# Four gate rows: products and copies replaced by a DMA round trip, and two chunks of the modulation summed later

## The reference

```python
mod = (c_act @ ada_w[layer] + ada_b[layer])[:, None, :]
sh_a, sc_a, gt_a, sh_m, sc_m, gt_m = jnp.split(mod, 6, axis=-1)
h = modulate(rms_norm(x, attn_norm[layer]), sh_a, sc_a)
...   # mix = diff_attention (layer 0) or nsa_attention, the sparse one (layer 1)
x = x + gt_a * mix
h = modulate(rms_norm(x, mlp_norm[layer]), sh_m, sc_m)
x = x + gt_m * squared_relu_mlp(h, mlp_w1[layer], mlp_w2[layer])
```

## Time and profile before

| | |
|---|---|
| median of 3 runs | 1310.14 us (1309.81 to 1311.36) |
| the profiled execution | 1312.58 us, span 1310.8 us |
| busy share PE / DVE / ACT / POOL | 96% / 66% / 53% / 10% |
| `m0` | about 172 to 343 us |
| sparse attention, blocks 0 to 18 | about 430 to 515 us |
| DMA | 267.38 MB, mean 204 GB/s |

### The profile page before, as it was taken

How to read it: one execution, slowest core, us unless ns; L and a number is a source line. 1 busy time by engine, 2 the same in 40 slices (tenths; PEclk the granted TensorE clock), 3 DMA queues, 4 the chain that set the end, 5 groups by cost and what they waited for, 6 DMA issues and landing times.

```text
span 1310.8 us, 21652 instructions
## 1 busy us (share of the span) xinstructions
PE 1262.0 (96%) x8368; PEld 1095.4 (84%) x8368; DVE 860.9 (66%) x1501; ACT 691.7 (53%) x1219; POOL 137.1 (10%) x154
## 2 busy tenths in 40 slices
PE   7999899999999999999999989999999999999999
PEld 5887799888799656899898867999998778899997
DVE  6588699997675675786546774665565566654444
ACT  3566553444455665645445874644444565654542
POOL 1022111211100000101100320100100100010100
PEclk9999999999999999999999999999999999999999
DMA  9979379999489142585553532685554554466550
GB/s 366 388 240 346 120 274 353 356 352 347 137 244 288 50 177 65 184 319 181 191 172 108 176 94 81 158 315 183 172 181 141 176 178 137 154 184 198 179 161 33
DMA packets 123781, 267.38 MB, mean 204 GB/s; under 512 B 11040, under 2 KB 33824, under 8 KB 123296
## 3 DMA queue, kind: packets, MB, share of 16 engines
q1 hardware_dynamic: 119328, 257.23, 59.2%
q0 software_dynamic: 1728, 6.29, 1.5%
q10 hardware_dynamic: 2624, 2.49, 0.6%
HBM read 264.83 MB, written 1.15 MB: 203 GB/s over the span
## 4 chain that ended last, share of the span: by engine, by line
PE 63%; DVE 5%; ACT 3%; issue 2%; POOL 1%; DVEq 0%; ACTq 0%; POOLq 0%
PE bank L538 12%; PE bank L540 11%; PE bank L539 11%; PE ps_s L538 3%; PE ps_s L539 3%; PE ps_s L540 3%; PE ps_p L539 3%; PE ps_p L538 3%; PE ps_p L540 3%; PE ps_s L1326 1%; DVE wlo L1621 1%; PE ps_p L1169 1%; PE ps_p L1145 1%; POOL rs L3446 1%; PE ps_s L1133 1%
## 5 line engine op out<-in xcount | busy, mean ns | idle before, releaser
L1621 DVE TENSOR_TENSOR wlo<-wring,whi 128x1024 fp32r<-128x1024 f32 (+1 forms) x376 | 457.9, 1227 | 265.4 <-ACT whi L2767 261.0
L2767 ACT ACTIVATE whi<-wring 128x1024 fp32r<-128x1024 f32 (+1 forms) x376 | 388.3, 1045 | 364.0 <-PE bank L540 132.2
L538 PE MATMUL bank<-h_hi,whi 128*128 128x256 f32 (+1 forms) x1224 | 348.8, 285 | 5.7 <-DVE wlo L1621 2.6
L539 PE MATMUL bank<-h_lo,whi 128*128 128x256 f32 (+1 forms) x1224 | 346.2, 283 | 0.0
L540 PE MATMUL bank<-h_hi,wlo 128*128 128x256 f32 (+1 forms) x1224 | 346.1, 283 | 0.0
L538 PEld LDWEIGHTS bank<-h_hi,whi 128*128 128x128 f32 (+1 forms) x1224 | 234.0, 191 | 11.9 <-issue 10.1
L539 PEld LDWEIGHTS bank<-h_lo,whi 128*128 128x128 f32 (+1 forms) x1224 | 234.1, 191 | 0.8
L540 PEld LDWEIGHTS bank<-h_hi,wlo 128*128 128x128 f32 (+1 forms) x1224 | 234.1, 191 | 0.0
L3462 POOL TENSOR_TENSOR ex<-ex 128x512 f32<-128x512 f32 x64 | 82.1, 1285 | 670.7 <-ACT g_hi L2898 670.5
L538 PE MATMUL ps_s<-whi,g_hi 128*128 128x512 f32 x256 | 101.2, 395 | 2.5 <-DVE wlo L1621 2.5
L538 PE MATMUL ps_p<-whi,g_hi 128*128 128x512 f32 x256 | 100.5, 393 | 0.0
(11 more groups left out here) (391 smaller groups left out, 1773.5 us busy)
## 6 DMA issues: line engine op xcount, KB each, us to landing
wring<-in_mlp_w SPq DMA_DIRECT2D x128, 512.0 KB, 5.3
wring<-in_mlp_w_in SPq DMA_DIRECT2D x64, 512.0 KB, 3.8
wring<-in_mlp_w_out SPq DMA_DIRECT2D x64, 512.0 KB, 4.1
wring<-in_ada_w_t SPq DMA_DIRECT2D x48, 512.0 KB, 8.0
wring<-in_ada_w SPq DMA_DIRECT2D x36, 512.0 KB, 5.8
wring<-in_moba_w_qkv SPq DMA_DIRECT2D x24, 512.0 KB, 4.0
wring<-in_a_qk SPq DMA_DIRECT2D x16, 512.0 KB, 9.2
wring<-in_kv_ada_w_t SPq DMA_DIRECT2D x16, 512.0 KB, 7.4
```

Source lines behind the costliest of these rows:

```text
L538: nc.tensor.matmul(out, lh, rh, start=first, stop=False, skip_group_check=mixed)
L539: nc.tensor.matmul(out, lh, rl, start=False, stop=False, skip_group_check=mixed)
L1621: v.tensor_tensor(piece_view(wlo, p), raw_view(p), piece_view(whi, p).bitcast(F32), ALU.subtract).then_inc(lo_ready, 1)
L2767: a.activation(piece_view(whi, p), raw_view(p), ACT.Copy).then_inc(hi_ready, 1)
```

## The change

It has two parts.

1. **The gate rows.** The products of `gate_rows` and the copies are gone from PE, DVE and ACT. In their place ACT issues `gate_out`: a DMA of the 8 columns of `mod`, 32 bytes from each of 128 partitions, to a DRAM scratch of 128 x 8 numbers. POOL issues `gate_load`: a DMA that reads the scratch as one run of 1024 numbers and writes it to all 128 partitions of `gate_row` (512 KB). The row then lies in the order (p, j), feature 128 j + p at place 8 p + j. `residual` and `y_residual` read it as `q (p j) -> q j p`: 4 runs of 128 numbers that stand 32 bytes apart.
2. **Two chunks moved.** The chunks 4 and 5 of `ada1` (the gate of the sparse attention) leave the list of weights of `m0` and DVE's pieces 40 to 47 there. They come as eight single loads between the loads behind `b_in`, and DVE sums the blocks in the sparse attention: two in block 0, one in each of the blocks 1 to 6, behind the block's weighting. Their neighbours are laid out anew: before, the list has four loads of `b_out`, eight of `ada_by_rows`, four of `b_out`; now two of `b_out`, the eight in halves among the sums' loads, then the rest.

```diff
-    plan += mix(mlp("m0"), ada(0, range(10, 12)) + ada("kv", range(4)) + ada(1, range(6)))
+    plan += mix(mlp("m0"), ada(0, range(10, 12)) + ada("kv", range(4)) + ada(1, range(4)))
...
-    for tag, lo, hi in (("b_out", 0, 2), ("b_out_mid", 2, 3), ("b_out_end", 3, 4)):
-        plan += [((tag, c[0][1]),) + c[1:4] + (c[4][lo:hi],) for c in b_out]
-        plan += ada_by_rows(1, range(8, 10)) if lo == 0 else []
+    gate_parts = [c[:4] + (c[4][j:j + 1],) for c in ada(1, range(4, 6)) for j in range(4)]
+    row_halves = [c[:4] + (c[4][j:j + 2],) for c in ada_by_rows(1, range(8, 10)) for j in (0, 2)]
...
+    plan += gate_parts[:2] + out_part["b_out", 0] + gate_parts[2:4]
+    for i in range(4):
+        plan += row_halves[i:i + 1] + (out_part["b_out", 1] if i == 3 else []) + gate_parts[4 + i:5 + i]
+    plan += [c for tag in ("b_out_mid", "b_out_end") for i in range(2) for c in out_part[tag, i]]
...
-        drain_order = [ada_order[c] for c in opening + CHUNKS[:2] + ROWS[:1] + CHUNKS[2:] + ROWS[1:]] + ada_order[10:]
+        drain_order = [ada_order[c] for c in opening + CHUNKS[:2] + ROWS[:1] + CHUNKS[2:] + ROWS[1:]] + ada_order[10:20]
+        drain_order += ada_order[22:24] + ada_order[20:22] + ada_order[24:]
...   # PE: gate_rows and its four calls are gone
...   # DVE
+            def gate_half(n):
+                return gate_row[:, :].rearrange("q (p j) -> q j p", j=KT)[:, 4 * n:4 * n + 4, :]
...
-                    v.tensor_tensor(tmp[:, n, :], src, gate_row[:, n * W:(n + 1) * W], ALU.mult).then_inc(drained[b], 1)
+                    v.tensor_tensor(tmp[:, n, :].rearrange("q (j p) -> q j p", p=P), src.rearrange("q (j p) -> q j p", p=P),
+                                    gate_half(n), ALU.mult).then_inc(drained[b], 1)
...
             def gate_use(name):
-                for g in range(2):
-                    bank_emptied(dve, (name, "gate", g))
+
+                dve.wait_ge(sem("gate_in"), 16 * (GATES.index(name) + 1))
...
-            mlp("m0", ada_order[10:22], last=lambda: (gate("m0"), gate_use("m0")))
+            mlp("m0", ada_order[10:20], last=lambda: gate_use("m0"))
...   # blocks of the sparse attention, behind nsa_weigh
+                for n in range(b + (b > 0), b + 2 if b < 7 else 0):
+                    matvec(ada_order[20 + n // 4], n % 4)
-                if b == 4:
-                    gate("n1")
...   # ACT: at b == 7 of m0 and m1, in slot 7 of a0, at b == 10 of the sparse attention
+            def gate_out(name):
+
+                first = gate_column[name]
+                act.wait_ge(mod_drained, drained_by(first // 4, first // 4 + 1))
+                a.dma_start(gate_scratch[GATES.index(name)], mod[:, first:first + KT]).then_inc(sem("gate_out"), 16)
...   # POOL: before the square 9 of m0 and m1, behind the roots of ("diff", 6) and ("kv", 1)
+            def gate_load(name):
+
+                i = GATES.index(name)
+                pool.wait_ge(sem("gate_out"), 16 * (i + 1))
+                if i:
+                    pool.wait_ge(x_ready, 4 * i)
+                g_.dma_start(gate_row[:, :], gate_scratch[i:i + 1].rearrange("a p j -> a (p j)").to_broadcast(
+                    [P, D])).then_inc(sem("gate_in"), 16)
```

More of the change, by code:

```diff
@@ L620, in by_token @@
                     piece_over(last, uses_[1] if end else None)
-            def gate_rows(name, first):
-                pe.wait_ge(mod_drained, drained_by(first // 4, first // 4 + 1))
-                for g in range(2):
[L626 to L633, removed]
             def attention(name, units, q_parts, pairs, v, dv, beside=None):
@@ L1047, in turn_inside @@
                     turn_scaled("kv", 0)
-            mlp("m0", lambda: gate_rows("m0", 40), inside=turn_inside)
+            mlp("m0", inside=turn_inside)
             late_rows(3)
@@ L1314, in turn_second @@
                 return step
-            mlp("m1", before_last=lambda: gate_rows("m1", 64 + 40), inside=turn_first("l", 12))
+            mlp("m1", inside=turn_first("l", 12))
             def head_scores(name, u, parts):
@@ L1901, in y_residual @@
                 if gated:
-                    link(v.tensor_tensor(tmp[:, n, :], y, gate_row[:, n * W:(n + 1) * W], ALU.mult))
+                    link(v.tensor_tensor(tmp[:, n, :].rearrange("q (j p) -> q j p", p=P), y.rearrange("q (j p) -> q j p", p=P),
+                                         gate_half(n), ALU.mult))
                     settle()
@@ L2456, in bias_steps @@
                         drained[uses[("bias2", s)][0]], 1)
-            mlp("m1", ada_order[26:28], other=late_constants, last=lambda: (gate("m1"), gate_use("m1")), first=8)
+            mlp("m1", ada_order[26:28], other=late_constants, last=lambda: gate_use("m1"), first=8)
             dve.wait_ge(sem("final_in"), 16)
@@ L2888, in mlp @@
                 for b in range(2 * FF // W):
+                    if b == 7 and tag in GATES:
+                        gate_out(tag)
                     key = (f"{tag}_w1", b // 2, b % 2)
@@ L3016, in _ @@
                 if s == 7:
-                    for g in range(2):
-                        drain(("a0", "gate", g), gate_row[:, g * W:(g + 1) * W], (0, W))
+                    gate_out("a0")
                 if slot_head(s - 3) is not None:
@@ L3127, in _ @@
                     q_drain(3)
+                if b == 10:
+                    gate_out("n1")
                 if b in (5, 7):
@@ L3456, in chunk_load @@
                 g_.dma_start(chunk_buffers[n % 2], src).then_inc(sem(f"chunk_in{n % 2}"), 16)
+            def gate_load(name):
[5 more added lines that the diff above has]
+                    [P, D])).then_inc(sem("gate_in"), 16)
             def squares(tag):
                 for b in range(2 * FF // W):
+                    if b == 9 and tag in GATES:
+                        gate_load(tag)
                     pool.wait_ge(sem("mlp_ghi"), 16 * int(tag[1]) + b + 1)
@@ L3471, in _ @@
                 roots(k)
+                if k == rstd_at[("diff", 6)]:
+                    gate_load("a0")
+                if k == rstd_at[("kv", 1)]:
+                    gate_load("n1")
                 if rstd_at[("diff", 0)] <= k < rstd_at[("diff", 4)]:
```

14 lines of the change are left out of this document (5 added, 9 removed).

## The result

| | before | changed |
|---|---|---|
| median | 1309.97 us (4 runs, 1308.57 to 1311.36) | 1326.50 us (4 runs, 1324.50 to 1327.61) |
| ratio | 1 | 1.0125, 95% interval 1.0104 to 1.0146 |
| profiled execution | 1312.58 us, span 1310.8 | 1324.50 us, span 1322.7 |

The change makes the kernel 16.5 us slower; the forecast was 1309.2 with a range from 1303.0 to 1317.5. I explain the 11.9 from the traces and let the medians of the experiments speak for the rest.

What follows compares the result with a forecast made beforehand. The prediction took PE as the bound (busy 96% of the span, 63% of the chain of waits). Its terms, -5.5 - 3.1 + 7.7 = -0.9, gave 1311.7 against 1312.6 profiled, 1309.2 against the median; range 1303.0 to 1317.5.

Steps and rivals of the forecast that it cites:

- Gate products and copies: `a0`, `m0`, `m1`: removed gate calls give 1.9, 1.7 and 1.7 us, DVE's copies 0.2; 5.5 us less.
- The DMA round trip: Gate write and load: taken as 0, since rows are wanted long after; in `m0`'s full queue 1.5 us more waiting.
- What `m0` gets back: Last third of `m0`: fewer loads and sums remove waits and slow clock, 4.6 less 1.5 for the gate load; 3.1 us less.
- What the sparse attention pays: Sparse attention: first blocks, late loads, slow clock, last sum and a DMA issue; 7.7 us more in all.
- Blocks 0 to 4: Sparse attention: the removed gate call gives 1.7, the sums cost 1.3 and 0.8 of lag; net +0.4 us.
- The wait at block 4: End of block 4, sparse attention: ACT's splits wait for later-issued `b_out` loads; PE goes on 4.8 us later, +0.4 included.
- the clock ... I take 1.5 for both: Sparse attention: slow clock behind PE's standing in block 1 to 2 and block 5; 1.5 us, range 0 to 3.6.
- Nothing in blocks 5 and 6 gives it back: Sparse attention: PE is the path on both sides, so the delay from block 4 stays.
- The last sum in block 6: Sparse attention: the sum stands between the weighting and the low part PE's mix needs; 1.2 us more.
- Strided reads: The 16 gated products: DVE reading `gate_row` 32 bytes apart costs nothing; 0 us, judged from L2240's PSUM read.
- The rival: Gated products: the strided read costs a pass, 0.56 us on 13 of 16, 7.3 in all, giving 1316.5; chance 0.24.

Runs made afterwards that it cites:

- e6: Only the first part (gates by DMA in 32-byte runs, chunks stay in `m0`), read contiguously so features get other features' gates; 1304.72 us, ratio 0.9958 to the kernel before.
- e2: Only the first part, with the scratch written in feature order by 4-byte writes so DVE reads contiguously; 1315.55 us, ratio 1.0036 to the kernel before.
- e7: Whole change, strided, `b_out`'s loads early as in e4, and the last two sums moved from blocks 5 and 6 to 7 and 8; 1311.86 us, ratio 1.0016.
- e1: Only the first part of the change: gates by DMA in 32-byte runs, read strided, weights list and sums as before; 1312.61 us, ratio 1.0020 to the kernel before.
- e12: As e7, but the gate row read contiguously (gates of other features); 1307.27 us, ratio 0.9979 to the kernel before.
- e3: The whole change with the scratch written by 4-byte writes so the row is read contiguously; 1326.32 us, ratio 1.0124 to the kernel before.
- e5: The whole change, written in 32-byte runs but read contiguously (gates of other features); 1317.75 us, ratio 1.0051 to the kernel before.
- e9: The whole change, each gate read at another distance: 16 bytes in `a0`, 64 in `m0`, 8 in `n1`, 128 in `m1`; 1321.59 us, ratio 1.0085.
- e4: The whole change, strided, with two loads of `b_out` placed ahead of the eight loads of rows; 1319.26 us, ratio 1.0075 to the kernel before.
- e8: Whole change, strided, loads around `b_out` listed as before, the eight sums in blocks 8 to 15, gate written at block 16; 1312.24 us, ratio 1.0020.
- e10: First part alone, PE turning gate columns to rows, ACT copying and writing 512-byte runs, contiguous reads; 1315.28 us, ratio 1.0034 to the kernel before.
- e11: As e10, with ACT's two copies in `m0` and `m1` moved behind the activations of block 8; 1307.18 us, ratio 0.9979 to the kernel before.

## Why the prediction was wrong

**Gate products and copies** (forecast -5.5): right. The calls gave 2.05, 1.9 and 1.5 us, and e6, 5.3 under the kernel before, has this term, the call of `n1` and the gate's load in it.

**The DMA round trip** (0, and 1.5 in `m0`): right for runs of 32 bytes; no product waited for its row; the 1.5 was not measured by itself. I had bounded the write by a few us of lateness. What it can cost was elsewhere: with 4-byte runs it held the queue of `m0` for 8 us (e2).

**What `m0` gets back** (-3.1): right in the trace, -3.4 between 241.84 and 307.95. But e7 is no better than e1 by more than 0.8, and e12 no better than e6, so in the median it hardly reached the end.

**What the sparse attention pays** (+7.7): the mechanism was right and its size was not. Blocks 0 to 4 (+0.4) were right: PE lost 2.1 us to the sums and the call gave 1.6 back. The wait at block 4 is as forecast (4.7 of ACT, 5.1 of PE between blocks 2 and 5, against 4.8). The step that failed is "the clock ... I take 1.5 for both": it is 5.4, since PE ran 12 us at half its clock behind the wait. e3, e5 and e9 have a like wait (5.0 to 5.5 us) and lose 5 to 6 us by the clock behind it. I had scaled it from the 1.8 behind a wait of 1.95, where the slow stretch is short, to a wait of 4.9. The bound that I gave from above, 3.6, was too low as well. "Nothing in blocks 5 and 6 gives it back" held. The last sum in block 6 (+1.2) did not show, since PE was late by then anyhow; when e4 took the first wait away it came up as a wait of 5.1, because its load was late, where I had priced its work alone.

**Strided reads** (0): wrong, and the largest error: 8 to 9 us by e5 and e6. The step that failed is "I take 0", by the row that was nearest, L2240, which reads PSUM. It was no neighbour: another memory. The rival had the right mechanism and nearly the right price (0.56 a product, measured 0.42 to 0.45; 7.3 in all, measured 8.8), and 0.24 for it was too little, since its only counter-evidence was that row. Its total is close in part by luck: 13 products of 0.42 to 0.45 are only 5.5 to 5.9 us, and the clock behind the products, which it left out, makes up more where it falls: 1.5 us behind each of two residuals in the changed kernel, none there in e1.

The Trainium skill's page that the prediction cites was the better guide. Page "SBUF — State Buffer", section "Specifications (TRN2)", asks for at least two hits in a line of 16 bytes for full bandwidth. Here the traces agree: at 8 bytes two numbers fall into a line and the product takes 0.69, at 16 one does and it takes 1.07. The note in section "Door 1: The DMA port swizzle", which the prediction drew on and which calls a distance of four fp32 numbers free, doesn't agree with the 1.07.

**The sum.** With 8.8 for the stride and 5.4 for the clock the forecast's own terms give 1309.2 + 8.8 + 3.9 = 1321.9. The rest to 1326.5, 4.6 us, I can't place in full. If the 3.1 of `m0` is left out, since it hardly reached the end in the median, the terms give 1325.0. And 1.6 us in the changed kernel's trace are a stretch of half clock in the latent attention (0.57 from 796 to 800 us). e2, e3, e5, e7, e8 and e10 have such a stretch some 20 to 30 us earlier in the same stage; e1, e4, e6, e9, e11, e12 and the kernel before have none. Nothing in that stage was changed. What starts it stays open.

## What to carry to other kernels

A row bounds an operand only in its own memory: where the layout of an SBUF operand changes and no row shows it, give the skill's rule for that memory the larger chance, or measure the one instruction first. Where a change reorders an in-order load queue, look for each load that moved behind a later release, and for what stands behind the engine that wants it; price a wait of PE of 5 us at one and a half times to twice its length (5.1 became 7.5 in e4, and about 10 in the changed kernel). When an experiment takes a cost away by another route, look whether that route has a price of its own before its time is read as a verdict.

## What the runs showed of the hardware

- DVE, 128 x 512 fp32, one operand in PSUM and one in SBUF: 0.69 us with numbers 4 or 8 bytes apart in SBUF, 1.07 at 16, 1.11 at 32, 1.02 to 1.04 at 64, 1.10 at 128 (e6, e9, changed kernel).
- 1024 writes of 4 bytes to DRAM from one DMA: 8 us in which all 16 engines together move 37 GB/s in place of 371, and loads beside it land after 12 us. 128 writes of 32 bytes: nothing to be seen. The Trainium skill, page "DMA: Bandwidth & Descriptors", section "Specifications", wants 512 bytes for the full rate. The trace of e2 agrees with it; the 32-byte runs are below that as well and show no cost in e6, perhaps because they are so few, which no run separates.
- A wait of PE of 4.9 us was followed by 12 us at 1.2 GHz, which cost 5.4, more than the wait; in e5, after 5.1 us, the clock did the same. In e4, after 5.1 us two blocks later, the clock's part was only about 2.
